# The last part of each query tile's difference goes to GpSimd

## The chip, the cores and the metric

The kernel runs on one core of a Trainium2 chip. The metric is the device time of one execution in microseconds (us). The page and the trace come from one profiled execution. TensorE multiplies and transposes (it writes PSUM alone), VectorE and ScalarE compute element by element in SBUF and PSUM, GpSimd computes in SBUF, and SyncE issues most of the DMAs.

## The reference, cut to what matters

A trunk of two layers over 2048 tokens of width 1024, all in float32: layer 0 runs differential attention (4 heads) and a sliding-window attention side by side, layer 1 a chunked attention. The change lies in the differential attention:

```python
def block(args):                       # one query tile of 128 tokens
    ...
    s = jnp.einsum('bhmqd,bhmkd->bhmqk', qi, k,
                   preferred_element_type=jnp.float32) * ATTN_SCALE + bias
    p = jax.nn.softmax(jnp.where(allowed, s, -jnp.inf), axis=-1)
    attn = p[:, :, 0] - lam * p[:, :, 1]
    return jnp.einsum('bhqk,bhkd->bhqd', attn.astype(v.dtype), v)
```

Each head has two maps m = 0 and 1 of 64 channels each. Their softmaxes are subtracted with the weight lam, and the difference is multiplied with v (128 channels). A query tile i sees the key tiles 0 to i.

## The kernel before, in words

`trunk` runs the stages one after the other: `prepare`, `project`, `diff_attn`, `band_attn` and `output` for layer 0, then `project`, `band_attn` and `output` for layer 1. Each engine has its own instruction list in a stage, and the lists meet at semaphores alone. The change touches `diff_attn`, which lies at 649 to 1090 us of the trace.

`steps` counts the pairs (head h, query tile i) as g = 0 to 63, 16 for each of 4 heads. The row of i + 1 key tiles is cut in two ways. `parts[g, m]` cuts it from the end for the logits, so that the last part holds up to 4 tiles (512 columns) that end on the diagonal. `turns[g]` cuts it from the start in groups of 4 tiles for the difference, the transposes and the product with v, so that the last group holds 1 to 4 tiles. Both have 1 part for i = 0 to 3, 2 for 4 to 7, 3 for 8 to 11 and 4 for 12 to 15.

Round g does the following on each engine, in the order written here.
- TensorE: logits of map 0 (`qk`, L632, two matmuls a part; a part waits until the exponential five parts back has left its PSUM buffer, L629), the product with v of tile g - 2 (`pv`, L658), logits of map 1, then the transposes of tile g - 1 (L645). The transposes of a group wait for its difference (L641) and for one of two PSUM buffers to be emptied (L643).
- VectorE: the minima of map 0 (the logits are negated; L700 for all parts but the last, L707 over these, and L711, which adds the bias to the last part and ends the minimum), the difference of tile g - 1, the minima of map 1, and the output of tile g - 2 (L730).
- ScalarE: the exponentials of map 0 with their sums (L764), the copies of the transposed groups of tile g - 1 to SBUF (L772), the exponentials of map 1, and the squares of tile g - 3 (L778).
- GpSimd: two memsets at the start of the stage (L612, L616), then nothing.

The difference (`difference`, L714 to L726) forms the row sums (L719), their reciprocals (L720) and `ratio`, the number by which map 1 is scaled against map 0 (L721). Then one scalar_tensor_tensor for each group reads both maps from SBUF and writes prob0 + ratio x prob1 over prob0 (L725). The buffers `prob` exist twice, for even and odd g.

Outside this stage GpSimd splits weights into a high and a low part: a cast (L332, L936) and a subtraction (L334, L938). VectorE's L447 is a scalar_tensor_tensor from two SBUF tensors, and L79 and L80 are tensor_tensor operations on one column.

Of the kernel before, what the change touches and what calls it, by code (L numbers as in the profile page):

```python
# [22 lines left out]
ALU = mybir.AluOpType  # L23
# [3 lines left out]
P = 128  # L27
# [496 lines left out]
def diff_attn(nc, before, keep, scr):  # L524

    with ExitStack() as ctx:
# [14 lines left out]
        part_sum = st.sb("part_sum", [P, 2, 2, 4])  # L542
        row_sum = st.sb("row_sum", [P, 2])
        inv_sum = st.sb("inv_sum", [P, 4, 2])
        ratio = st.sb("ratio", [P, 1])
        RING = 5
        logits = [st.ps(f"logits{i}", [P, BLK]) for i in range(RING)]
        turned = [st.ps(f"turned{i}", [P, BLK]) for i in range(2)]
        o_ps = st.ps("o", [P, P])
        head_loaded = [st.sems(f"head_loaded{b}_", NBLK) for b in range(2)]  # L550
        bias_loaded, flipped, bias_made, mask_set, chain = (st.sem(x) for x in ("bias_loaded", "flipped", "bias_made", "mask_set", "chain"))
        qk_done, max_done, exp_done, diff_done, turned_done, prob_t_done, pv_done, out_done, sq_done = (
            st.sem(x) for x in ("qk_done", "max_done", "exp_done", "diff_done", "turned_done", "prob_t_done", "pv_done", "out_done", "sq_done"))
        mean_done, root_done, norm_done, norm_turned, norm_out, stored = (
            st.sem(x) for x in ("mean_done", "root_done", "norm_done", "norm_turned", "norm_out", "stored"))
        LOADS = 13
# [17 lines left out]
        for g, (h, i) in enumerate(steps):  # L574
            turns[g] = []
            for at in range(0, i + 1, TPB):
                turns[g].append((group, at, min(TPB, i + 1 - at)))
                group += 1
        G = len(steps)

        block = ctx.enter_context(nc.Block())

# [26 lines left out]
        @block.gpsimd  # L609
        def _(pool):  # L610
            st.clear_before(pool)
            nc.gpsimd.memset(bias[:, :, 0:BLK - NEAR], 0.0).then_inc(mask_set, 1)  # L612
            pool.wait_ge(mask_set, 1)

            pool.wait_ge(bias_made, A_HEADS // 2)
            nc.gpsimd.memset(bias[0:HD, :, BLK - HD:BLK], MASKED).then_inc(mask_set, 1)  # L616

        @block.tensor
        def _(pe):
            def qk(g, m, k):  # L620

                h, i = steps[g]
                if k >= len(parts[g, m]):
                    return
                if m == 0 and k == 0 and i % TPB == 0:
                    pe.wait_ge(head_loaded[h % 2][i // TPB], 16 * LOADS * (h // 2 + 1))
                n, at, tiles = parts[g, m][k]
                if n >= RING:
                    pe.wait_ge(exp_done, n - RING + 1)  # L629
                for s in range(2):  # L630
                    q = q_sb[h % 2][m][s][:, i * P:(i + 1) * P]
                    last = nc.tensor.matmul(logits[n % RING][:, 0:tiles * P], q, k_sb[h % 2][m][:, at * P:(at + tiles) * P],  # L632
                                            start=s == 0, stop=s == 1)
                last.then_inc(qk_done, 1)

            def transposes(g, k):

                if k >= len(turns[g]):
                    return
                n, at, tiles = turns[g][k]  # L640
                pe.wait_ge(diff_done, n + 1)  # L641
                if n >= 2:
                    pe.wait_ge(prob_t_done, n - 1)  # L643
                for t in range(tiles):
                    last = nc.tensor.transpose(turned[n % 2][:, t * P:(t + 1) * P], prob[g % 2][0][:, (at + t) * P:(at + t + 1) * P], keep["ident"][:, :])  # L645
                last.then_inc(turned_done, 1)

            def pv(g, k):

                h, i = steps[g]  # L650
                if k >= len(turns[g]):
                    return
                n, at, tiles = turns[g][k]
                pe.wait_ge(prob_t_done, n + 1)
                if k == 0 and g >= 1:
                    pe.wait_ge(out_done, g)
                for t in range(at, at + tiles):
                    last = nc.tensor.matmul(o_ps[:, :], prob_t[:, g % 2, t * P:(t + 1) * P], v_sb[:, h % 2, t, :], start=t == 0, stop=t == i)  # L658
                if k == len(turns[g]) - 1:
                    last.then_inc(pv_done, 1)  # L660

            pe.wait_ge(bias_loaded, 16)
            for n in range(A_HEADS // 2):
                nc.tensor.matmul(turned[n % 2][:, :], keep["flip"][:, :], bias_raw[:, 2 * n:2 * n + 2, :], start=True, stop=True).then_inc(flipped, 1)
            pe.wait_ge(bias_made, A_HEADS // 2)
            for g in range(G + 2):
                for k in range(NBLK if g < G else 0):
                    qk(g, 0, k)
                for k in range(NBLK if g >= 2 else 0):
                    pv(g - 2, k)  # L670
                for k in range(NBLK if g < G else 0):
                    qk(g, 1, k)
                for k in range(NBLK if 1 <= g <= G else 0):
                    transposes(g - 1, k)
            for n in range(A_HEADS * NBLK):
                pe.wait_ge(norm_done, TPB * (n + 1))
                if n >= 2:
                    pe.wait_ge(norm_out, n - 1)
                for t in range(TPB):
                    last = nc.tensor.transpose(turned[n % 2][:, t * P:(t + 1) * P], out[:, n * TPB + t, :], keep["ident"][:, :])  # L680
                last.then_inc(norm_turned, 1)

        @block.vector
        def _(dve):
# [29 lines left out]
            def difference(g):  # L714

                h, i = steps[g]
                k = len(parts[g, 0])
                dve.wait_ge(exp_done, parts[g, 1][-1][0] + 1)
                link(nc.vector.reduce_sum(row_sum[:, :], part_sum[:, g % 2, :, 0:k], AX.X))  # L719
                link(nc.vector.reciprocal(inv_sum[:, g % 4, :], row_sum[:, :]))  # L720
                link(nc.vector.scalar_tensor_tensor(out=ratio[:, :], in0=row_sum[:, 0:1], scalar=keep["nlam"][:, 0:1],  # L721
                                                    in1=inv_sum[:, g % 4, 1:2], op0=ALU.mult, op1=ALU.mult))
                for n, at, tiles in turns[g]:
                    cols = slice(at * P, (at + tiles) * P)
                    nc.vector.scalar_tensor_tensor(out=prob[g % 2][0][:, cols], in0=prob[g % 2][1][:, cols], scalar=ratio[:, 0:1],  # L725
                                                   in1=prob[g % 2][0][:, cols], op0=ALU.mult, op1=ALU.add).then_inc(diff_done, 1)  # L726

            def output(g):
# [24 lines left out]
        @block.scalar  # L753
        def _(act):
            def exponentials(g, m):
                j = (2 * g + m) % 4
                act.wait_ge(max_done, 2 * g + m + 1)
                if g >= 2:
                    if m == 0:
                        act.wait_ge(turned_done, turns[g - 2][-1][0] + 1)  # L760
                    else:
                        act.wait_ge(diff_done, turns[g - 2][-1][0] + 1)
                for k, (n, at, tiles) in enumerate(parts[g, m]):
                    nc.scalar.activation(prob[g % 2][m][:, at * P:(at + tiles) * P], logits[n % RING][:, 0:tiles * P], ACT.Exp,  # L764
                                         bias=neg_max[:, j:j + 1], scale=-1.0, accum_out=part_sum[:, g % 2, m, k:k + 1]).then_inc(exp_done, 1)

            def leave(g):
                if g >= 2:
                    act.wait_ge(pv_done, g - 1)
                for n, at, tiles in turns[g]:  # L770
                    act.wait_ge(turned_done, n + 1)
                    nc.scalar.activation(prob_t[:, g % 2, at * P:(at + tiles) * P], turned[n % 2][:, 0:tiles * P], ACT.Copy).then_inc(prob_t_done, 1)  # L772

            def squares(g):
                act.wait_ge(out_done, g + 1)
                if g >= 1:
                    act.wait_ge(sq_done, g)
                nc.scalar.activation(square[:, :], out[:, g, :], ACT.Square, accum_out=ssq[:, g:g + 1]).then_inc(sq_done, 1)  # L778

            for g in range(G + 3):  # L780
                if g < G:
                    exponentials(g, 0)
                if 1 <= g <= G:
                    leave(g - 1)
                if g < G:
                    exponentials(g, 1)
                if g >= 3:
                    squares(g - 3)
            act.wait_ge(mean_done, 1)
            nc.scalar.activation(root[:, :], mean[:, :], ACT.Sqrt).then_inc(root_done, 1)  # L790
            for n in range(A_HEADS * NBLK):
                h, b = divmod(n, NBLK)
                act.wait_ge(norm_turned, n + 1)
                nc.scalar.activation(prob[h // 2][h % 2][:, b * BLK:(b + 1) * BLK], turned[n % 2][:, :], ACT.Copy,
                                     scale=keep["sub_g"][:, 0:1]).then_inc(norm_out, 1)
# [541 lines left out]
```

## Time and profile before

| what | value |
| --- | --- |
| median of 3 runs | 2934.63 us (2934.42 to 2936.46) |
| the profiled execution's own time | 2935.31 us |
| its span in the trace | 2933.6 us |
| mean granted TensorE clock | 0.969 of full speed |
| busy: TensorE matmuls | 2656.7 us (91%) |
| busy: VectorE | 1154.5 us (39%) |
| busy: ScalarE | 1019.0 us (35%) |
| busy: GpSimd | 307.9 us (10%) |

The span runs from the first to the last instruction of the program; the profiled execution's own time is 1.7 us longer. The busy shares are means over stages with different limits: in the first attention VectorE is busy for some 86 us of each 100, in the projections it is nearly idle. Matmuls are pipelined and the ends of their rows are modelled, so a busy TensorE need not be one at its peak. Busy spans of GpSimd are rough.

### The profile page before, as it was taken

Reading aid. Unit: us, or ns where it says so; the run is one execution under the profiler, and the core shown is the slowest. Engines: PE = TensorE matmul, PEld = TensorE weight load, DVE = VectorE, ACT = ScalarE, POOL = GpSimd, SP = SyncE. Lnnn points to the kernel's source line nnn. Section 1 sums busy time; section 2 is a strip of 40 time slices with the busy share of each in tenths; the row PEclk is TensorE's granted clock in tenths of the full one; section 3 lists DMA queues with packets and bytes.
Section 4 is the critical chain, followed back from the end, with each engine's and each line's share of the span. In section 5 each row is a group of like instructions: output and inputs, shape, how many; then the busy total and the mean of one; then the engine's idle time right before and its main releaser. Section 6 shows DMA issues by size and latency. Waiting matters only on the chain. (4 is left out here: it accounts for less than half of the span.)

```text
span 2933.6 us, 44852 instructions
## 1 busy us (share of the span) xinstructions
PE 2656.7 (91%) x16292; PEld 2252.2 (77%) x16292; DVE 1154.5 (39%) x2983; ACT 1019.0 (35%) x2516; POOL 307.9 (10%) x193
## 2 busy tenths in 40 slices
PE   3999999988888876679969999999996999999898
PEld 2788888986677655558858888888995888888687
DVE  5411111108889865445531111111101555555465
ACT  3211111006777754432221111111001777777221
POOL 1121212100000002110011122122100000100100
PEclk9999999999999998889979999999997999999899
DMA  4433322129414028866563433322216677875552
GB/s 140 128 123 107 122 79 82 50 68 182 101 29 74 1 89 188 184 184 225 190 204 108 129 123 114 101 79 70 68 47 154 127 155 156 165 145 123 183 202 85
DMA packets 235396, 358.27 MB, mean 122 GB/s; under 512 B 63464, under 2 KB 132756, under 8 KB 234692
## 3 DMA queue, kind: packets, MB, share of 16 engines
q1 hardware_dynamic: 225140, 316.95, 41.0%
q0 software_dynamic: 10064, 38.80, 4.5%
q8 instruction: 116, 1.90, 0.3%
q14 instruction: 76, 0.62, 0.1%
HBM read 222.45 MB, written 133.21 MB: 121 GB/s over the span
## 5 line engine op out<-in xcount | busy, mean ns | idle before, releaser
L509 PE MATMUL p_acc<-p_h_hi,p_w_hi 128*128 128x512 f32 x1440 | 566.5, 393 | 16.1 <-DVE p_h_lo L457 16.1
L509 PE MATMUL p_acc<-p_h_lo,p_w_hi 128*128 128x512 f32 x1440 | 563.2, 391 | 0.0
L509 PE MATMUL p_acc<-p_h_hi,p_w_lo 128*128 128x512 f32 x1440 | 563.0, 391 | 0.0
L509 PEld LDWEIGHTS p_acc<-p_h_hi,p_w_hi 128*128 128x128 f32 x1440 | 272.0, 189 | 74.6 <-DVE p_h_lo L457 19.4
L509 PEld LDWEIGHTS p_acc<-p_h_hi,p_w_lo 128*128 128x128 f32 x1440 | 271.7, 189 | 56.8
L509 PEld LDWEIGHTS p_acc<-p_h_lo,p_w_hi 128*128 128x128 f32 x1440 | 272.0, 189 | 55.3
L1034 DVE CUSTOM_DVE_ANT_0 c_logits<-c_logits,c_bias 128x640 f32<-128x640 f32 (+4 forms) x256 | 191.5, 748 | 228.7 <-PE c_logits L961 220.7
L305 DVE SCALAR_TENSOR_TENSOR p_lo_out<-p_acc,p_hi_out 128x512 fp32r<-128x512 f32 x116 | 80.2, 691 | 498.3 <-ACT p_hi_out L289 498.3
L289 ACT ACTIVATE p_hi_out<-p_acc 128x512 fp32r<-128x512 f32 x116 | 69.4, 598 | 513.6 <-PE p_acc L509 513.5
L506 PE MATMUL p_acc<-p_w_hi,p_h_lo 128*128 128x256 f32 (+1 forms) x768 | 224.3, 292 | 0.0
L506 PE MATMUL p_acc<-p_w_lo,p_h_hi 128*128 128x256 f32 (+1 forms) x768 | 224.3, 292 | 0.0
L506 PE MATMUL p_acc<-p_w_hi,p_h_hi 128*128 128x256 f32 (+1 forms) x768 | 224.3, 292 | 0.0
L1262 PE MATMUL o_acc<-w_out_hi,o_m_hi 128*128 128x512 f32 x512 | 204.4, 399 | 6.7 <-DVE o_m_lo L1213 6.7
L764 ACT ACTIVATE a_prob<-a_logits,a_neg_max 128x512 f32<-128x512 f32 (+3 forms) x320 | 195.8, 624 | 41.7 <-DVE a_neg_max L711 40.3
L961 PE MATMUL c_logits<-c_k,c_q 128*128 128x384 f32 (+2 forms) x960 | 202.0, 330 | 8.8 <-DMA c_v<-scr_v 6.8
L1262 PE MATMUL o_acc<-w_out_lo,o_m_hi 128*128 128x512 f32 x512 | 201.5, 394 | 0.0
L1262 PE MATMUL o_acc<-w_out_hi,o_m_lo 128*128 128x512 f32 x512 | 201.3, 393 | 0.0
L632 PE MATMUL a_logits<-a_k,a_q 128*128 128x512 f32 (+3 forms) x640 | 175.3, 395 | 27.1 <-ACT a_prob L764 18.4
L1074 ACT ACTIVATE c_prob<-c_logits,c_neg_max 128x640 f32<-128x640 f32 (+4 forms) x256 | 186.2, 727 | 30.8 <-DVE c_neg_max L1034 30.6
L1063 ACT ACTIVATE c_prob_t<-c_turned 128x512 f32<-128x512 f32 (+3 forms) x256 | 141.5, 553 | 115.3 <-PE c_turned L970 115.2
L961 PEld LDWEIGHTS c_logits<-c_k,c_q 128*128 128x128 f32 x960 | 152.9, 191 | 31.7 <-issue 19.0
L988 PE MATMUL c_o<-c_prob_t,c_v 128*64 128x128 f32 x2240 | 168.4, 278 | 8.0 <-DVE c_prob_t L1048 6.5
(161 smaller groups left out, 4036.3 us busy)
## 6 DMA issues: line engine op xcount, KB each, us to landing
scr_qh<-p_hi_out SPq DMA_DIRECT2D x116, 256.0 KB, 2.5
scr_ql<-p_lo_out SPq DMA_DIRECT2D x116, 256.0 KB, 2.9
scr_gt<-p_f_out SPq DMA_DIRECT2D x128, 128.0 KB, 1.9
p_w_raw<-in_w_in_odd POOLq DMA_DIRECT2D x16, 1024.0 KB, 6.7
c_q<-scr_qh SPq DMA_DIRECT2D x64, 256.0 KB, 8.0
c_q<-scr_ql SPq DMA_DIRECT2D x64, 256.0 KB, 9.8
o_o<-scr_ot SPq DMA_DIRECT2D x6, 2048.0 KB, 9.2
o_g<-scr_gt SPq DMA_DIRECT2D x6, 2048.0 KB, 15.0
```

Of the source, the lines that this page charges most:

```text
L289: nc.scalar.activation(hi_out[:, buf, :], ps[:, :], ACT.Copy, scale=kind[1]).then_inc(act_done, 1)
L305: nc.vector.scalar_tensor_tensor(out=lo_out[:, buf, :], in0=ps[:, :], scalar=kind[1], in1=hi_out[:, buf, :].bitcast(F32), op0=ALU.mult, op ...
L506: last = nc.tensor.matmul(acc[v % 4][:, 0:n], ht[:, c, k * P:(k + 1) * P], wt[:, half, c * n:(c + 1) * n], **flags)
L509: last = nc.tensor.matmul(acc[v % 4][:, :], wt[:, half, c * n + cc * P:c * n + (cc + 1) * P], ht[:, c, b * BLK:(b + 1) * BLK], **flags)
L632: last = nc.tensor.matmul(logits[n % RING][:, 0:tiles * P], q, k_sb[h % 2][m][:, at * P:(at + tiles) * P], start=s == 0, stop=s == 1)
L764: nc.scalar.activation(prob[g % 2][m][:, at * P:(at + tiles) * P], logits[n % RING][:, 0:tiles * P], ACT.Exp, bias=neg_max[:, j:j + 1], sc ...
L961: last = nc.tensor.matmul(s_ps[:, lo:hi], q_sb[b][s][:, i * P:(i + 1) * P], k_sb[b][:, tile * P:tile * P + hi - lo], start=s == 0, stop=s ...
L988: last = nc.tensor.matmul(o_ps[half * HD:(half + 1) * HD, at:at + P], v_sb[:, j // TILES % 2, tile_of(j + half) - w + 1 + t, :], prob_t[:, ...
L1034: nc.vector.tensor_tensor_reduce(out=to, in0=s, in1=bias[:, b, WIDE - w * P:WIDE + SPARE], scale=1.0, scalar=HIGHEST, op0=ALU.add, op1=ALU ...
L1063: nc.scalar.activation(prob_t[:, j % 4, 0:n], turned[j % 2][:, 0:n], ACT.Copy).then_inc(main_copied, 1)
L1074: nc.scalar.activation(prob[:, j, 0:n], source, ACT.Exp, bias=neg_max[:, j:j + 1], scale=-1.0, accum_out=sums[:, h, tile_of(k):tile_of(k) ...
L1262: last = nc.tensor.matmul(acc[u % 4][:, :], mt[:, t % 2, c, :], wt[:, c, half * BLK:(half + 1) * BLK], start=step == 0, stop=step == 3 * K ...
```

## The change

For every query tile with more than one group (i = 4 to 15, 48 of 64 tiles), the last group of the difference is no longer formed by VectorE. GpSimd waits for the ratio and the last exponential, scales its columns of map 1 in place by the ratio, waits for its own result, and adds them to map 0. `ratio` gets two columns, one for even and one for odd g, and its writing signals `ratio_set`, on which VectorE waits as well in place of `chain`. The last group's transposes wait for `pool_diff_done`, the others for `diff_done`, whose count is taken over VectorE's groups alone (`owned`). VectorE waits before it writes the ratio, and ScalarE before it writes map 1, for GpSimd's difference of two tiles ago.

```diff
-        ratio = st.sb("ratio", [P, 1])
+        ratio = st.sb("ratio", [P, 2])
...
+        shared = [g for g in range(G) if len(turns[g]) > 1]
+
+        def alone(g):
+            return turns[g][:-1] if g in shared else turns[g]
+
+        owned = {g: sum(len(alone(e)) for e in range(g + 1)) for g in range(G)}
+        lent = {g: sum(e <= g for e in shared) for g in range(G)}
...
             nc.gpsimd.memset(bias[0:HD, :, BLK - HD:BLK], MASKED).then_inc(mask_set, 1)
+            for g in shared:
+                n, at, tiles = turns[g][-1]
+                cols = slice(at * P, (at + tiles) * P)
+                pool.wait_ge(exp_done, parts[g, 1][-1][0] + 1)
+                pool.wait_ge(ratio_set, g + 1)
+                nc.gpsimd.tensor_scalar(prob[g % 2][1][:, cols], prob[g % 2][1][:, cols], ratio[:, g % 2:g % 2 + 1], None, ALU.mult).then_inc(pool_scaled, 1)
+                pool.wait_ge(pool_scaled, lent[g])
+                nc.gpsimd.tensor_tensor(prob[g % 2][0][:, cols], prob[g % 2][0][:, cols], prob[g % 2][1][:, cols], ALU.add).then_inc(pool_diff_done, 1)
...
-                pe.wait_ge(diff_done, n + 1)
+                if g in shared and k == len(turns[g]) - 1:
+                    pe.wait_ge(pool_diff_done, lent[g])
+                else:
+                    pe.wait_ge(diff_done, owned[g] - len(alone(g)) + k + 1)
...
-                link(nc.vector.scalar_tensor_tensor(out=ratio[:, :], in0=row_sum[:, 0:1], scalar=keep["nlam"][:, 0:1],
-                                                    in1=inv_sum[:, g % 4, 1:2], op0=ALU.mult, op1=ALU.mult))
-                for n, at, tiles in turns[g]:
+                if g >= 2 and lent[g - 2] > 0:
+                    dve.wait_ge(pool_diff_done, lent[g - 2])
+                scaled_by = ratio[:, g % 2:g % 2 + 1]
+                nc.vector.scalar_tensor_tensor(out=scaled_by, in0=row_sum[:, 0:1], scalar=keep["nlam"][:, 0:1],
+                                                    in1=inv_sum[:, g % 4, 1:2], op0=ALU.mult, op1=ALU.mult).then_inc(ratio_set, 1)
+                dve.wait_ge(ratio_set, g + 1)
+                for n, at, tiles in alone(g):
...
-                        act.wait_ge(diff_done, turns[g - 2][-1][0] + 1)
+                        act.wait_ge(diff_done, owned[g - 2])
+                        if lent[g - 2] > 0:
+                            act.wait_ge(pool_diff_done, lent[g - 2])
```

## Rows read from the trace of the kernel before

**Rows 1.** Busy time by engine (x instructions) in stretches: tiles 5 and 13.

```profile
core 0: us, PE busy (x) PEld busy (x) DVE busy (x) ACT busy (x) POOL busy (x), PEclk, DMA share, GB/s
784.40:789.00 4.60, 4.08 (x27) 3.15 (x26) 4.41 (x15) 3.83 (x14) 0.00 (x0) 1.00 0.82 219
840.60:851.00 10.40, 8.94 (x59) 7.08 (x58) 8.72 (x23) 7.49 (x22) 0.00 (x0) 1.00 0.00 1
```

**Rows 2.** Timeline, tile 13: start, length, engine, line, operation, [idle before <- releaser].

```profile
845.80 0.90 PE L645 MATMUL a_turned<-keep_ident,a_prob 128*128 128x128 f32 x6 [0.68 <-ACT a_prob_t L772]
...
847.95 0.30 PEld L632 LDWEIGHTS a_logits<-a_k,a_q 128*128 128x128 f32 x2 [1.22 <-ACT a_prob L764]
```

**Rows 3.** Timeline, difference of tile 6 of the second head and what follows.

```profile
789.40 0.22 DVE L721 SCALAR_TENSOR_TENSOR a_ratio<-a_row_sum,keep_nlam,a_inv_sum 128x1 f32<-128x1 f32 x1
789.65 1.28 DVE L725 SCALAR_TENSOR_TENSOR a_prob<-a_prob,a_ratio 128x512 f32<-128x512 f32 x2
...
790.46 0.84 PEld L645 LDWEIGHTS a_turned<-keep_ident,a_prob 128*128 128x128 f32 x7 [0.55 <-DVE a_prob L725]
...
791.29 1.40 PE L632 MATMUL a_logits<-a_k,a_q 128*128 128x128 f32 x6
...
792.42 0.69 ACT L764 ACTIVATE a_prob<-a_logits,a_neg_max 128x512 f32<-128x512 f32 x1 [0.23 <-DVE a_neg_max L711]
...
792.51 0.88 DVE L700 TENSOR_REDUCE a_part_max<-a_logits 128x1 f32<-128x128 f32 x2
...
793.61 0.76 DVE L711 CUSTOM_DVE_ANT_0 a_logits<-a_logits,a_bias,a_part_max 128x512 f32<-128x512 f32 x1
```

**Rows 4.** Timeline, difference of tile 7 of the second head and what follows.

```profile
794.94 1.42 DVE L725 SCALAR_TENSOR_TENSOR a_prob<-a_prob,a_ratio 128x512 f32<-128x512 f32 x2
...
796.41 0.42 PEld L645 LDWEIGHTS a_turned<-keep_ident,a_prob 128*128 128x128 f32 x4 [0.24 <-DVE a_prob L725]
...
798.23 0.37 ACT L764 ACTIVATE a_prob<-a_logits,a_neg_max 128x128 f32<-128x128 f32 x1 [0.53 <-DVE a_neg_max L711]
...
798.74 0.74 PE L632 MATMUL a_logits<-a_k,a_q 128*128 128x512 f32 x2 [0.96 <-ACT a_prob L764]
...
799.63 0.76 DVE L711 CUSTOM_DVE_ANT_0 a_logits<-a_logits,a_bias,a_part_max 128x512 f32<-128x512 f32 x1
```

**Rows 5.** Timeline, difference of tile 15 of the second head, third head's start.

```profile
861.25 2.74 DVE L725 SCALAR_TENSOR_TENSOR a_prob<-a_prob,a_ratio 128x512 f32<-128x512 f32 x4
...
863.55 1.23 PE L645 MATMUL a_turned<-keep_ident,a_prob 128*128 128x128 f32 x8 [0.18 <-ACT a_prob_t L772]
...
864.21 1.20 ACT L772 ACTIVATE a_prob_t<-a_turned 128x512 f32<-128x512 f32 x2 [0.21 <-PE a_turned L645]
...
865.31 0.36 ACT L764 ACTIVATE a_prob<-a_logits,a_neg_max 128x128 f32<-128x128 f32 x1
```

**Rows 6.** Timeline in the first projection, where GpSimd and VectorE meet.

```profile
42.33 1.28 DVE L447 SCALAR_TENSOR_TENSOR p_x<-p_x,p_inv,p_g 128x1024 f32<-128x1024 f32 x1
43.36 2.01 POOL L332 CAST p_w_hi<-p_w_raw 128x2048 fp32r<-128x2048 f32 x1 [7.66 <-DMA p_w_raw<-in_w_in_even]
...
45.45 4.50 POOL L334 TENSOR_TENSOR p_w_lo<-p_w_raw,p_w_hi 128x2048 fp32r<-128x2048 f32 x1
...
47.89 2.08 DVE L79 TENSOR_TENSOR p_root<-p_inv 128x1 f32<-128x1 f32 x1
50.01 0.16 DVE L80 TENSOR_TENSOR p_root<-p_root,p_mean 128x1 f32<-128x1 f32 x1
```

**Rows 7.** Groups of GpSimd by shape: busy, mean ns of one, idle before.

```profile
L334 POOL TENSOR_TENSOR p_w_lo<-p_w_raw,p_w_hi 128x2048 fp32r<-128x2048 f32 x24 | 110.3, 4594 | 2.1
L332 POOL CAST p_w_hi<-p_w_raw 128x2048 fp32r<-128x2048 f32 x24 | 45.5, 1895 | 828.1 <-PE p_acc L509 739.8 <-PE p_acc L506 75.4 <-DMA p_w_raw<-in_w_in_even 7.7
L938 POOL TENSOR_TENSOR w_out_lo<-c_w_raw,w_out_hi 128x1024 fp32r<-128x1024 f32 x8 | 18.9, 2357 | 0.7
...
L1132 POOL COPY o_wide<-o_inv_sums 128x512 f32<-128x512 f32 x16 | 9.8, 614 | 169.3 <-PE o_spread L1247 140.5 <-remote 28.8
```

More of the change, by code:

```diff
@@ L551, in diff_attn @@
         bias_loaded, flipped, bias_made, mask_set, chain = (st.sem(x) for x in ("bias_loaded", "flipped", "bias_made", "mask_set", "chain"))
-        qk_done, max_done, exp_done, diff_done, turned_done, prob_t_done, pv_done, out_done, sq_done = (
-            st.sem(x) for x in ("qk_done", "max_done", "exp_done", "diff_done", "turned_done", "prob_t_done", "pv_done", "out_done", "sq_done"))
+        qk_done, max_done, exp_done, ratio_set, pool_scaled, pool_diff_done, diff_done, turned_done, prob_t_done, pv_done, out_done, sq_done = (
+            st.sem(x) for x in ("qk_done", "max_done", "exp_done", "ratio_set", "pool_scaled", "pool_diff_done", "diff_done", "turned_done", "prob_t_done", "pv_done", "out_done", "sq_done"))
         mean_done, root_done, norm_done, norm_turned, norm_out, stored = (
@@ L720, in difference @@
                 link(nc.vector.reciprocal(inv_sum[:, g % 4, :], row_sum[:, :]))
-                link(nc.vector.scalar_tensor_tensor(out=ratio[:, :], in0=row_sum[:, 0:1], scalar=keep["nlam"][:, 0:1],
-                                                    in1=inv_sum[:, g % 4, 1:2], op0=ALU.mult, op1=ALU.mult))
-                for n, at, tiles in turns[g]:
+                if g >= 2 and lent[g - 2] > 0:
[5 more added lines that the diff above has]
+                for n, at, tiles in alone(g):
                     cols = slice(at * P, (at + tiles) * P)
-                    nc.vector.scalar_tensor_tensor(out=prob[g % 2][0][:, cols], in0=prob[g % 2][1][:, cols], scalar=ratio[:, 0:1],
+                    nc.vector.scalar_tensor_tensor(out=prob[g % 2][0][:, cols], in0=prob[g % 2][1][:, cols], scalar=scaled_by,
                                                    in1=prob[g % 2][0][:, cols], op0=ALU.mult, op1=ALU.add).then_inc(diff_done, 1)
```

## The prediction

> **What bounds the kernel now.** I read the page first: the chain that ended last lies in the last output stage and says nothing of the first attention. So I took the busy time of each engine in stretches as long as one query tile of that attention, then the timeline of single tiles, always asking which engine starts the next piece without having waited. A "step" i below is the stretch after the difference of query tile i; it has ceil((i+1)/4) parts, and its last part has 1 to 4 tiles.
>
> The stage has two regimes. In the two-part steps VectorE is nearly full: 4.41 of 4.60 us [rows 1]. In the four-part steps it is not: 8.72 of 10.40 us [rows 1]. There TensorE waits for ScalarE, which has to empty the two transpose buffers and then free a logits buffer [rows 2]; the last part's difference is ready long before its turn. So a difference that VectorE finishes earlier can be worth something in short steps only, and one that comes ready later hurts where TensorE is already waiting for it: in the two-part steps (0.55 and 0.24 us [rows 3, 4]) and behind tile 15 of a head, where the next head's tile is small and nothing else is left to do.
>
> **What VectorE gets rid of.** 12 tiles of a head (i = 4 to 15) lose their last part. Two parts in a row, the last of 384 columns, take 1.28 us, and with 512 columns 1.42 [rows 3, 4]; four of 512 take 2.74 [rows 5]. So one of 512 costs (2.74 - 1.42)/2 = 0.66 us of slot, one of 384 0.52, and by the same slope 256 and 128 cost 0.39 and 0.26. That is 3 x (0.66 + 0.52 + 0.39 + 0.26) = 5.5 us a head, 22 us in all.
>
> **What GpSimd takes for it.** No row shows its tensor_scalar. From below it costs what the one-input copies cost: 0.614 us at 512 columns and 1.895 at 2048 [rows 7], so 0.83 ns a column over 0.19: 0.61, 0.51, 0.40, 0.29 us for 4 to 1 tiles. From above it costs a tensor_tensor. That has two inputs: 2.357 us at 1024 and 4.594 at 2048 [rows 7], so 2.18 ns a column over 0.12: 1.24, 0.96, 0.68, 0.40 us. I take the copy's price, since the operation has one input tensor as well. Between the two instructions lie 0.08 us (43.36 + 2.01 to 45.45 [rows 6]). The sum is 1.93, 1.55, 1.16, 0.77 us for 4 to 1 tiles. 
>
> **When GpSimd can start.** Both engines wait for the same ratio. VectorE's own next operation starts 0.25 us after the ratio's start [rows 3]; GpSimd cannot be earlier by more than a few hundredths. The rows then show that the two don't run side by side. VectorE's tensor_tensor of one column took 2.08 us instead of the 0.16 of its neighbour, and ended at 49.97, with GpSimd's tensor_tensor that had begun before it and ended at 49.95 [rows 6]. The other way, GpSimd's cast took 2.01 us instead of 1.895 when it began under a scalar_tensor_tensor that reads two SBUF tensors [rows 6, 7], the very form of the difference. In both cases the second one ran as if it had started 0.14 us before the first one's end. So I take it that of a difference on VectorE and an operation on GpSimd the later waits for the earlier. The Trainium skill says so too (SBUF — State Buffer, "Who interferes with whom"): a VectorE instruction with two SBUF inputs and a GpSimd instruction that reads SBUF exclude each other for the whole instruction. It adds that issue order decides who blocks; what happens when a third instruction queues up is shown by no row here.
>
> One part of 512 lasts 0.75 us (1.42 - 0.66 [rows 4]). VectorE's first part begins at 0; GpSimd's scaling then runs from 0.61 on.
>
> **Two-part steps (i = 4 to 7).** VectorE has only that one part, so GpSimd goes on undisturbed and is ready at 0.61 + 0.77, 1.16, 1.55, 1.93 = 1.38, 1.77, 2.16, 2.54 us. VectorE was ready at 1.02, 1.15, 1.28, 1.42, the first two by the slope of the slots and the others from [rows 3, 4]. The last transposes come 0.36, 0.62, 0.88 and 1.12 us later, while VectorE itself arrives earlier at its next maxima and waits there.
> - i = 6 [rows 3]: ready at 789.65 + 2.16 = 791.81. Three weight loads of 0.12 (0.84/7) bring TensorE to the next logits at 792.2 instead of 791.29; its second pair ends about 793.15; a maximum over 512 columns and the small one behind it bring VectorE to its last maximum at 794.1 instead of 793.61: +0.48. So 0.40 of the 0.88 us is covered.
> - i = 5 and 4 have the same order of work; with the same cover 0.62 gives +0.22 and 0.36 gives nothing.
> - i = 7 [rows 4]: ready at 794.94 + 2.54 = 797.48; transposes, copy and with it the exponentials start 0.55 later (798.78 instead of 798.23, since four transposes and a copy need 1.3 us). The logits that wait for the first of them move from 798.74 to 799.29 and end at 800.03 instead of 799.48. VectorE's last maximum, which stood 0.15 behind them at 799.63, can begin at 800.06: +0.43.
>
> Sum of a head +1.13, four heads +4.5 us.
>
> **Steps of three and four parts.** GpSimd finishes before the transposes want it: those of the last part wait for the buffer [rows 2]. The one gain is in step 8, the last one in which VectorE still leads: its slot of 0.26 less a wait of some 0.1 for GpSimd's scaling. I take -0.2 a head, -0.8 us in all. In steps 12 to 14 GpSimd gets between VectorE's parts and costs VectorE 0, 0.3 and 0.54 us net, worked out as for tile 15 below, which its 1.7 idle us of such a step [rows 1] hide; without that cover it would be +0.8 a head.
>
> **Behind tile 15.** Four parts become three on VectorE. If the one that waits first goes first, the order is part, scaling, part, addition, part: scaling ready at 0.61 + 0.61 = 1.22, second part from 1.08 to 1.83, addition from 1.69 to 2.93, third part from 2.79 to 3.54. Before, the third part was ready at 0.75 + 2 x 0.65 = 2.05. Its transposes began at 863.55 and its copy at 864.21 [rows 5], 0.66 apart; now they begin at 861.25 + 3.54 + 0.04 = 864.83, the copy at 865.49: +1.28 us. The fourth follows at once. The next head's exponentials (865.31 [rows 5]) stand behind these copies on ScalarE, and the product with v behind them on TensorE: +1.28 for all that follows, four times +5.1 us.
>
> **The added waits.** VectorE's for the GpSimd difference of two tiles ago, with its own parts and maxima queued behind it, and ScalarE's likewise, fall a whole step (4 us or more) after that difference is done: nothing. GpSimd has nothing else queued in this stage.
>
> **Sum.** 4.5 - 0.8 + 5.1 = +8.8 us. The profiled execution's 2935.3 would become 2944.1; against the median of 2934.6 that is 2943.4 us.
>
> **Rivals.**
> - VectorE keeps the lock between its parts, as its next part is issued before the last has drained. Then GpSimd starts after all of VectorE's parts. The two-part steps are the same (+4.5), step 8 gives its whole 0.26 (-1.0); behind tile 15 the last part is ready at 2.05 - 0.14 + 1.93 = 3.84 instead of 2.74, of which the wait for a transpose buffer hides some 0.1: +1.0 a head, +4.0. Sum +7.5: 2942 us.
> - GpSimd's scaling costs as much as its addition. All of GpSimd's work is longer by 0.63, 0.45, 0.28, 0.11 us, nearly all of it in the open: about 0.1 + 0.3 + 0.45 + 0.6 + 0.65 and 0.3 in step 14, 2.4 a head, +9.5 us more: 2953 us.
> - Not slower: the two engines don't exclude each other for this pair of forms. GpSimd is then ready at 0.03 + 1.93 and so on, behind VectorE's old time by only 0.5 us or less, inside the cover of 0.40 or near it. Steps 4 to 7 then give only about 0.1 each, because the exponentials that the next ratio waits for follow ScalarE's copies and these start no earlier; step 8 gives 0.3 and the head's end 0.4: -1.1 a head, 2930.2 us, within 0.2%. It decides as soon as VectorE's parts keep their 0.66 us spacing with GpSimd busy. The lengthened rows speak against it.
> - Faster: VectorE bounds all steps and the whole 22 us come back: 2912 us. Its idle time in long steps and the waits of TensorE for it in short ones speak against it.
>
> **Chances.** Taking turns as summed 0.50, VectorE's parts first 0.20, dear scaling 0.15, no exclusion 0.10, whole gain 0.05. A measurement of this kernel tells from no change what is over about 0.2% (5.9 us). My terms are 1 us in 4, so the first two cases fall within 5.9 us three times in ten: same 0.21 + 0.09 = 0.30, faster 0.05, slower 0.65. The range leaves out the whole gain and most of no exclusion and reaches up to the dear scaling: 2936 to 2953.
>
> **What would show it.** In the changed profile: GpSimd's scaling of 512 columns ends 1.2 us after VectorE's first part began, not 0.65; in four-part steps VectorE's parts stand over 1 us apart; TensorE's wait before the transposes names GpSimd in steps 5 to 7 of each head and from tile 15's first part to the next head's exponentials it takes 5.3 us instead of 4.1 [rows 5]; the steps with three and four parts keep their length. It is wrong if those long steps get shorter, if the two engines' operations overlap at their usual lengths, or if GpSimd's two instructions at 512 columns last well over 2 us.

## The result and the profile after

The changed kernel takes 2955.61 us (median of 4 runs, 2952.96 to 2958.84) where the kernel before takes 2935.55 (2934.42 to 2936.89): ratio 1.007, 95% interval 1.0057 to 1.0083, so 20 us or 0.7% slower. The forecast was slower, 2943.4 us, range 2936 to 2953. The time lies outside the range, and the loss is more than twice the 8.8 us of the sum. The profiled execution took 2956.68 us, with a span of 2954.9.

In the two traces the first copy of the first attention on VectorE starts 1.6 us earlier than before, and the first matrix multiplication of the next stage 19.3 us later (1114.77, before 1095.52). No other stage changed its length by more than 1.6 us. To see where the loss arose, I took the starts of the row sum (L719 before, L737 after) as marks and compared the length of each step (mark of tile i to mark of tile i + 1) with the same step in the kernel before. The first row gives the length before in us, the others the difference:

| head, step i | 4 | 5 | 6 | 7 | 8 | 9 | 10 | 11 | 12 to 14 | 15 |
| --- | --- | --- | --- | --- | --- | --- | --- | --- | --- | --- |
| second head before | 4.23 | 4.64 | 5.30 | 6.02 | 6.51 | 6.88 | 8.19 | 9.09 | 29.6 | 5.20 |
| first | +0.23 | +0.77 | +1.37 | +1.49 | -0.17 | -0.05 | -0.11 | +0.02 | +0.05 | +0.82 |
| second | +0.22 | +0.76 | +1.22 | +1.46 | -0.13 | -0.05 | -0.09 | -0.02 | +0.03 | +0.82 |
| third | +0.23 | +0.76 | +1.22 | +1.98 | +0.36 | +0.07 | 0.00 | +0.01 | +0.06 | +0.81 |
| fourth | +0.23 | +0.77 | +1.23 | +1.97 | +0.72 | -0.10 | -0.07 | -0.03 | +0.03 | |

Steps 0 to 3 are unchanged to 0.01 us. The two-part steps bear 16 of the 18.9 us between the first mark and the last; of the rest of the stage's loss, 0.6 us lie before the first mark and 1.3 behind the last.

The groups of GpSimd in this stage, by shape (busy, mean ns of one, idle before):

```profile
L629 POOL TENSOR_SCALAR a_prob<-a_prob,a_ratio 128x512 f32<-128x512 f32 x12 | 24.3, 2022 | 62.5 <-ACT a_prob L788 36.6 <-DVE a_ratio L742 25.9
...
L631 POOL TENSOR_TENSOR a_prob<-a_prob 128x512 f32<-128x512 f32 x12 | 15.6, 1301 | 1.0
...
L629 POOL TENSOR_SCALAR a_prob<-a_prob,a_ratio 128x128 f32<-128x128 f32 x12 | 13.0, 1087 | 114.5 <-ACT a_prob L788 114.5
```

The scaling, forecast at 0.61 us for 512 columns, takes longer than the addition. The timeline of tile 7 of the second head, where [rows 4] stood:

```profile
800.59 0.75 DVE L747 SCALAR_TENSOR_TENSOR a_prob<-a_prob,a_ratio 128x512 f32<-128x512 f32 x1
800.73 2.05 POOL L629 TENSOR_SCALAR a_prob<-a_prob,a_ratio 128x512 f32<-128x512 f32 x1 [3.72 <-ACT a_prob L788]
...
802.86 1.26 POOL L631 TENSOR_TENSOR a_prob<-a_prob 128x512 f32<-128x512 f32 x1
...
804.17 0.42 PEld L663 LDWEIGHTS a_turned<-keep_ident,a_prob 128*128 128x128 f32 x4 [2.35 <-POOL a_prob L631]
...
805.11 1.16 DVE L718 TENSOR_REDUCE a_part_max<-a_logits 128x1 f32<-128x256 f32 x2 [1.72 <-PE a_logits L647]
805.36 0.36 ACT L788 ACTIVATE a_prob<-a_logits,a_neg_max 128x128 f32<-128x128 f32 x1
```

The last part is ready 3.53 us after VectorE's first part began (1.42 in [rows 4]); TensorE's weight loads stand idle for 2.35 us (0.24 before), and VectorE, freed 0.66 us earlier, waits 1.72 us for the logits behind those transposes. Tile 15 of the same head, against [rows 5]:

```profile
868.11 2.51 DVE L747 SCALAR_TENSOR_TENSOR a_prob<-a_prob,a_ratio 128x512 f32<-128x512 f32 x3
868.25 2.05 POOL L629 TENSOR_SCALAR a_prob<-a_prob,a_ratio 128x512 f32<-128x512 f32 x1 [6.48 <-DVE a_ratio L742]
868.92 0.42 PEld L663 LDWEIGHTS a_turned<-keep_ident,a_prob 128*128 128x128 f32 x4 [1.20 <-DVE a_prob L747]
...
870.01 0.42 PEld L663 LDWEIGHTS a_turned<-keep_ident,a_prob 128*128 128x128 f32 x4 [0.68 <-DVE a_prob L747]
...
870.38 1.37 POOL L631 TENSOR_TENSOR a_prob<-a_prob 128x512 f32<-128x512 f32 x1
...
871.80 0.42 PEld L663 LDWEIGHTS a_turned<-keep_ident,a_prob 128*128 128x128 f32 x4 [0.71 <-POOL a_prob L631]
...
872.99 0.36 ACT L788 ACTIVATE a_prob<-a_logits,a_neg_max 128x128 f32<-128x128 f32 x1
```

The first and second group of transposes are 1.09 us apart (868.92 and 870.01), not 0.66: VectorE's second part was held, which here means that it ended later than in the kernel before, by 0.43 us, and only by that, though the scaling went on until 870.30.

### The profile page after: what moved, and what is told of

The parts are those of the page before. It is cut to its first block and busy times, and to the rows that moved or that the text cites. A ratio compares the mean times of both kernels' runs of the same rounds, so it can differ in the third digit from the quotient of the medians.

```text
span 2954.9 us, 45009 instructions
## 1 busy us (share of the span) xinstructions
PE 2661.7 (90%) x16292; PEld 2256.1 (76%) x16292; DVE 1148.8 (39%) x2935; ACT 1020.3 (35%) x2516; POOL 428.8 (15%) x289
## 5 line engine op out<-in xcount | busy, mean ns | idle before, releaser
L332 POOL CAST p_w_hi<-p_w_raw 128x2048 fp32r<-128x2048 f32 (+2 forms) x27 | 51.0, 1887 | 931.4 <-PE p_acc L509 844.6
```

Of the source, the lines that this page charges most:

```text
L332: nc.gpsimd.tensor_copy(w_hi[:, s % 2, 0:KC * n], w_raw[:, 0:KC * n]).then_inc(w_hi_done, 1)
```

## The experiments

The first theory after the result: the loss is the late last part in two-part steps and at tile 15, late because the scaling is far dearer than a copy. The rival: VectorE and GpSimd exclude each other, and that is what costs, wherever both work. Kernels are compared with the kernel before in the same runs; its median there was 2937.5 us for the first four, 2934.4 for the next three and 2938.4 for the last.

**What the operations cost alone (e_bench).** `go` issues an operation and waits for its end.

```diff
+                for n in (1, 2, 3, 4):
+                    to, one, two = (trial[:, j, 0:n * P] for j in range(3))
+                    go(nc.gpsimd.tensor_scalar(one, one, scale[:, 0:1], None, ALU.mult))
+                    go(nc.gpsimd.tensor_tensor(to, one, two, ALU.add))
+                    go(nc.gpsimd.tensor_scalar(two, two, 1.0, None, ALU.mult))
+                    go(nc.gpsimd.tensor_copy(to, two))
+                    go(nc.gpsimd.tensor_tensor(one, one, scale[:, 0:1].to_broadcast([P, n * P]), ALU.mult))
```

> The kernel before, with 60 operations of GpSimd on scratch tiles added one after the other in the first stage, where VectorE does nothing that matters: its time as a whole is of no interest, only the length of each operation alone. Theory (the scaling itself is dear): in the changed kernel GpSimd's tensor_scalar by a column of factors ended 1.23, 1.54, 1.87, 2.19 us after VectorE's part began, and could start at 0.61; alone it should take about 0.61, 0.93, 1.25, 1.57 us for 1 to 4 tiles. Rival (the long rows are waits for VectorE, the operation costs as a copy does): 0.29, 0.40, 0.51, 0.61 us. Second rival (no wait is in them at all): 1.09, 1.41, 1.73, 2.05 us. tensor_tensor 0.40, 0.68, 0.96, 1.24 by all of them. Whether a factor that is a constant, or a multiplication by the factor column read as a tensor, is cheaper is open; the column read as a tensor should cost as a tensor_tensor, 1.24 us at 4 tiles.

Groups of GpSimd by shape in this run:

```profile
L172 POOL TENSOR_SCALAR prep_trial<-prep_trial,prep_scale 128x512 f32<-128x512 f32 x3 | 4.7, 1565 | 0.3
L174 POOL TENSOR_SCALAR prep_trial<-prep_trial 128x512 f32<-128x512 f32 x3 | 4.5, 1490 | 0.3
L173 POOL TENSOR_TENSOR prep_trial<-prep_trial 128x512 f32<-128x512 f32 x3 | 3.8, 1262 | 0.2
L172 POOL TENSOR_SCALAR prep_trial<-prep_trial,prep_scale 128x384 f32<-128x384 f32 x3 | 3.7, 1247 | 0.3
...
L176 POOL TENSOR_TENSOR prep_trial<-prep_trial,prep_scale 128x512 f32<-128x512 f32 x3 | 3.1, 1041 | 0.3
...
L172 POOL TENSOR_SCALAR prep_trial<-prep_trial,prep_scale 128x256 f32<-128x256 f32 x3 | 2.8, 924 | 0.3
...
L175 POOL COPY prep_trial<-prep_trial 128x512 f32<-128x512 f32 x3 | 1.8, 611 | 0.2
L172 POOL TENSOR_SCALAR prep_trial<-prep_trial,prep_scale 128x128 f32<-128x128 f32 x3 | 1.8, 605 | 0.3
```

The scaling alone takes 0.605, 0.924, 1.247 and 1.565 us, the theory's four numbers to 0.01. So 2.05 us in the changed kernel are 1.57 of work and 0.48 of waiting, from 0.14 after the start of VectorE's first part to 0.62: the wait behind that part was forecast right, the price was not. A constant factor is hardly cheaper (1.490). Multiplying two tensors is much cheaper (1.041), and cheaper than the 1.24 expected of it. The time of this kernel, 2980.11 us in one run, says nothing: the trial operations are in it.

**Which steps pay (e_two, e_long, e_edge).** Each hands over the last parts of some tiles only:

```diff
-        shared = [g for g in range(G) if len(turns[g]) > 1]
+        shared = [g for g in range(G) if 4 <= steps[g][1] < 8]    (e_two; e_long: 8 <= ... < 15; e_edge: ... == 15)
```

> GpSimd takes the last part of tiles 4 to 7 of each head alone, VectorE does tiles 8 to 15 whole. Theory (the loss is the late last part in the two-part steps): these steps grew by 0.23, 0.77, 1.3 and 1.5 us (2.0 where the TensorE clock fell), 16 to 17 us in four heads: 2951 to 2953 us. Rival (the loss is spread over all shared tiles, as VectorE is slowed by GpSimd wherever both work): 16 of 48 tiles, a third of the 20 us, 2942 us.

> GpSimd takes the last part of tiles 8 to 14 of each head alone. Theory: step 8 gains 0.15 us a head and the rest nothing, though VectorE's parts stand up to 0.43 us apart more: 2935 us, within 1.5 us of the kernel before. Rival (spread loss): 28 of 48 tiles, 2947 us. Rival of another kind (taking work off VectorE is a gain where nothing waits for GpSimd): its 28 parts of 0.26 to 0.66 us, 12 us, 2924 us.

> GpSimd takes the last part of tile 15 of each head alone. Theory: each head's end grows by 0.82 us, the last one perhaps by more: +3.3 to +4 us, 2939 us. Rival (spread loss): 4 of 48 tiles, 2937.5 us. By the sum of the prediction it would be +5.1 us.

| run | median us | ratio to before | 95% interval | marks, first to last |
| --- | --- | --- | --- | --- |
| e_two | 2952.01 | 1.0054 | 1.0036 to 1.0073 | +18.0 us |
| e_long | 2934.70 | 0.9994 | 0.9984 to 1.0003 | -0.8 us |
| e_edge | 2938.56 | 1.0009 | 0.9999 to 1.002 | +2.9 us |

Tiles 4 to 7 alone bring 0.54% of the 0.70%: 16 tiles, a third of those shared, most of the loss. In e_two their steps grow by 0.22, 0.77, 1.23 and 1.5 to 2.0 us as in the changed kernel, 15.8 of its 18.0 us; 1.6 of the rest lie in step 8, where GpSimd does nothing in this run, and 0.6 in one early step. Tiles 8 to 14 cost nothing and gain nothing that their time can tell; the marks of e_long show step 8 shorter by 0.15 us in three heads (longer by 0.09 in the fourth), steps 9 and 10 by 0.05 and 0.1 us. In e_edge tile 15 adds 0.82, 1.04 and 0.81 us in the three heads that have a mark behind it; the time of that run alone couldn't tell 2937.5 us from 2939. So "spread over all shared tiles" falls, and so does "work taken off VectorE is a gain where nothing waits for GpSimd".

**A cheaper scaling (e_add).**

```diff
-                nc.gpsimd.tensor_scalar(prob[g % 2][1][:, cols], prob[g % 2][1][:, cols], ratio[:, g % 2:g % 2 + 1], None, ALU.mult)...
+                nc.gpsimd.tensor_tensor(prob[g % 2][1][:, cols], prob[g % 2][1][:, cols], ratio[:, g % 2:g % 2 + 1].to_broadcast([P, tiles * P]), ALU.mult)...
```

> The changed kernel, with GpSimd's scaling written as a multiplication of two tensors, the second one the factor column repeated over the width. Theory (the length of GpSimd's two operations after VectorE's part is what the two-part steps pay): if this form costs 0.40, 0.68, 0.96, 1.24 us instead of 0.61, 0.93, 1.25, 1.57, the last part comes earlier by 0.21, 0.25, 0.29, 0.33 us, nearly all of it in steps 5 to 7 and at tile 15: about 1.1 to 1.4 us a head, 5 us in all, so 2950 to 2951 us where the changed kernel takes 2955.6. Rival (the lock on VectorE's second part is what counts): two inputs hold it longer, so this is no faster, 2955 us or more.

Measured: 2954.75 us, ratio 1.0067 (1.004 to 1.0094), which can't be told from the changed kernel; by the marks +16.7 us instead of +18.9. The two-part steps of the second head grow by 0.01, 0.45, 0.79 and 0.93 us (0.22, 0.76, 1.22, 1.46 in the changed kernel): each pays less by what the last part is earlier. But step 15 of the first head grows by 1.54 us instead of 0.82. An operation of GpSimd that reads two inputs holds VectorE's parts longer (second head):

```profile
864.16 3.87 DVE L747 SCALAR_TENSOR_TENSOR a_prob<-a_prob,a_ratio 128x512 f32<-128x512 f32 x3
864.27 1.54 POOL L629 TENSOR_TENSOR a_prob<-a_prob,a_ratio 128x512 f32<-128x512 f32 x1 [7.01 <-DVE a_ratio L742]
...
865.89 1.59 POOL L631 TENSOR_TENSOR a_prob<-a_prob 128x512 f32<-128x512 f32 x1
```

VectorE's three parts take 3.87 us here, 2.51 in the changed kernel. In the second and third heads step 15 grows by more, 2.37 and 1.69 us, and the step behind it by 0.73 and 1.40. There the granted clock fell to 1.2 GHz for 3.4 us (from 868.1 and 973.9), behind waits of TensorE of 1.0 us for VectorE's parts (columns as in [rows 1]):

```profile
864.00:868.00 4.00, 2.08 (x16) 1.47 (x14) 3.96 (x5) 1.31 (x4) 3.14 (x2) 1.00 0.00 2
868.00:872.00 4.00, 3.91 (x21) 3.91 (x22) 1.82 (x10) 2.29 (x8) 0.00 (x0) 0.57 0.00 0
```

Against the first head, where the clock stayed up, that is about 3.1 us of the 16.7. The two-part steps save 7.2 us in all, and tile 15 gives 3.2 of them back, part of it by the clock. So theory and rival are both right in kind, each in its steps, and the theory's 2950 to 2951 us missed what happens at tile 15.

**The exclusion by itself (e_shadow, e_fill).** VectorE forms all parts as before, and GpSimd works beside it on scratch tiles:

```diff
+        shade = st.sb("shade", [P, 2, BLK])
...
-                nc.gpsimd.tensor_scalar(prob[g % 2][1][:, cols], prob[g % 2][1][:, cols], ratio...
+                nc.gpsimd.tensor_scalar(shade[:, 1, 0:tiles * P], shade[:, 1, 0:tiles * P], ratio...    (e_fill: nc.gpsimd.memset(shade[:, 1, 0:tiles * P], 1.0))
...
-                for n, at, tiles in alone(g):
+                for n, at, tiles in turns[g]:
```

> VectorE forms every part itself, as in the kernel before, and nothing waits for GpSimd but the writing of the ratio two tiles later; GpSimd does its two operations at the same moments on scratch tiles. So this is the price of the contention alone. Theory (small): VectorE's second part is held 0.11, 0.22, 0.32, 0.43 us, as in the changed kernel, and its later ones by the addition; in two-part steps that delay is under the cover of 0.40 us, at tile 15 a few tenths stay open: 0 to +3 us, 2935 to 2938 us. Rival (contention is the loss): most of the 20 us, 2950 us.

> As the run with scratch tiles, but GpSimd writes constants instead: two operations that read nothing. If it is the reading that excludes VectorE's two-input operation, VectorE's parts keep their distance of 0.65 to 0.67 us in every step and the time is that of the kernel before, 2935 to 2936 us. If any operation of GpSimd excludes it, the second part is held here too, by up to 0.5 us.

e_shadow took 2953.05 us, ratio 1.0063 (1.0043 to 1.0083): my 0 to +3 us was far off. e_fill took 2933.18 us, ratio 0.9994 (0.9983 to 1.0004): these operations, which read nothing, cost nothing, and neither do the signals and waits around the ratio, which both runs keep. Tile 6 and tile 15 in e_shadow, then tile 15 in e_fill:

```profile
790.96 1.61 DVE L748 SCALAR_TENSOR_TENSOR a_prob<-a_prob,a_ratio 128x512 f32<-128x512 f32 x2
791.09 1.74 POOL L633 TENSOR_SCALAR a_shade<-a_shade,a_ratio 128x384 f32<-128x384 f32 x1 [2.61 <-DVE a_ratio L743]
...
864.60 4.19 DVE L748 SCALAR_TENSOR_TENSOR a_prob<-a_prob,a_ratio 128x512 f32<-128x512 f32 x4
864.73 2.06 POOL L633 TENSOR_SCALAR a_shade<-a_shade,a_ratio 128x512 f32<-128x512 f32 x1 [6.89 <-DVE a_ratio L743]
```

```profile
860.44 2.74 DVE L748 SCALAR_TENSOR_TENSOR a_prob<-a_prob,a_ratio 128x512 f32<-128x512 f32 x4
860.52 0.53 POOL L633 MEMSET a_shade<- 128x512 f32 x1 [8.73 <-DVE a_ratio L743]
```

The two parts of tile 6 take 1.61 us instead of 1.28 [rows 3], the four of tile 15 4.19 instead of 2.74 [rows 5]; under the memsets they keep 2.74. The memsets are shorter as well (0.53 us), but the first runs beside VectorE's first part and the second one, from 0.66 to 1.18 us, beside its second, and neither part shows it. e_shadow's profiled execution was its fastest, 14.4 us longer than before by the marks: 4.4 in the two-part steps, 5.8 in steps 8 to 14 and 4.1 at tile 15. By the marks the steps of the second head grow by 0.11, 0.23, 0.32, 0.42 (4 to 7), 0.31, 0.23, 0.21, 0.10 (8 to 11), 0.43 (14) and 1.37 us (15). In the two-part steps this is the hold of the second part, to 0.02 us. VectorE leads there, so its own delay is paid in full; the cover (what a step does not pay of a delay) of 0.40 us that I had applied belongs to a last part that comes late while VectorE itself is early. That is why the expectation was wrong, and the run doesn't contradict the others: the changed kernel has no second part on VectorE in those steps that could be held, and in the steps from 8 on the part that VectorE loses is as long as the hold or longer (0.26 to 0.66 against 0.11 to 0.43 us).

**A law for the two-part steps (e_tile).** In each two-part step take how much later the last part is ready than before, and what the step grows:

| step | ready before | changed: ready, growth | e_add: ready, growth | lateness less growth, both |
| --- | --- | --- | --- | --- |
| 4 | 1.02 | 1.77, 0.22 | 1.55, 0.01 | 0.53, 0.52 |
| 5 | 1.15 | 2.35, 0.76 | 2.03, 0.45 | 0.44, 0.43 |
| 6 | 1.28 | 2.94, 1.22 | 2.51, 0.79 | 0.44, 0.44 |
| 7 | 1.42 | 3.53, 1.46 | 2.99, 0.93 | 0.65, 0.64 |

Ready is counted in us from the start of VectorE's first part. With these two prices of GpSimd's work the cover of a step is the same. To test this forward, GpSimd got one key tile only:

```diff
-        shared = [g for g in range(G) if len(turns[g]) > 1]
+        shared = [g for g in range(G) if 4 <= steps[g][1] < 8]
...
-            return turns[g][:-1] if g in shared else turns[g]
+            if g not in shared:
+                return turns[g]
+            n, at, tiles = turns[g][-1]
+            return turns[g][:-1] + ([(n, at, tiles - 1)] if tiles > 1 else [])
...
-                cols = slice(at * P, (at + tiles) * P)
+                cols = slice((at + tiles - 1) * P, (at + tiles) * P)
...
+                    pe.wait_ge(diff_done, owned[g])
                     pe.wait_ge(pool_diff_done, lent[g])
```

> In tiles 4 to 7 of each head GpSimd takes one key tile (128 columns) of the last part and VectorE the 0 to 3 others; all other tiles are VectorE's alone. Theory (a two-part step grows by how much later its last part is ready than in the kernel before, less a fixed cover): GpSimd is ready 1.77 us after VectorE's first part began in all four steps, instead of 1.02, 1.15, 1.28 and 1.42; the changed kernel and the run with two tensors both gave covers of 0.52, 0.43, 0.44 and 0.64. So the steps should grow by 0.23, 0.19, 0.05 and 0 us, 1.9 us in four heads: 2937 us, a few tenths less for what VectorE is rid of. Rival (what GpSimd and VectorE do to each other's reads counts, whatever is late): VectorE's second part is held 0.11 us in three of the four steps, so each grows by about 0.11 more, and by less in step 4 than in step 7. Second rival (any work of GpSimd there costs as in the run with tiles 4 to 7 whole): 2952 us.

The steps grew by 0.24, 0.19, 0.06 and -0.03 us in the second head and by the same within 0.02 in the others: the law's four numbers. GpSimd's rows there (scaling, addition, by group):

```profile
L632 POOL TENSOR_SCALAR a_prob<-a_prob,a_ratio 128x128 f32<-128x128 f32 x16 | 17.4, 1085 | 314.2 <-ACT a_prob L792 289.9 <-DVE a_ratio L746 24.3
L634 POOL TENSOR_TENSOR a_prob<-a_prob 128x128 f32<-128x128 f32 x16 | 7.3, 454 | 1.3
```

The time was 2936.87 us, ratio 1.0003 (0.9991 to 1.0016): an unchanged time and the 1.9 us of the law (1.0006) both lie inside the interval, the rival's 2952 us far outside. The law rests on the marks, not on this ratio. The first rival is not put to the test by this run, because VectorE was not late in it. Its second part was held by 0.11 us, but it was shorter by one tile, and the two parts of tile 7 end no later than in [rows 4] (1.42):

```profile
793.72 1.39 DVE L751 SCALAR_TENSOR_TENSOR a_prob<-a_prob,a_ratio 128x512 f32<-128x512 f32 x2
```

What a delay of VectorE costs is shown by e_shadow.

**What is left.** Step 7 of the third and fourth heads grew by 1.98 instead of 1.46, and step 8 by 0.36 and 0.72 instead of -0.15. Busy time and granted clock around that step of the third head (columns as in [rows 1]):

```profile
905.00:909.00 4.00, 1.88 (x13) 1.30 (x12) 2.42 (x7) 1.64 (x6) 3.00 (x2) 1.00 1.09 201
909.00:913.00 4.00, 3.96 (x18) 3.04 (x17) 2.81 (x9) 3.35 (x12) 0.19 (x1) 0.57 1.08 226
913.00:917.00 4.00, 3.60 (x26) 2.99 (x24) 3.47 (x9) 2.69 (x8) 1.44 (x2) 1.00 0.32 59
```

TensorE was busy for 1.88 of the 4 us before, and from 909.2 the granted clock was at its lower level of 1.2 GHz for 3.4 us. It was so at three places in this stage of the changed kernel (694.1, 909.2 and 1015.0), behind waits for GpSimd of 1.5, 2.1 and 2.1 us, and at none in the kernel before between 674 and 1072. Step 7 of the second head had the same wait of 2.1 us and no fall, so the wait alone doesn't decide it. The extra is 1.0 us in the third head and 1.4 in the fourth, about 2.4 us in all, and 0.2 in the first. e_two repeats it: the clock fell in step 7 of its first and third heads (701.2 and 909.4), and there alone step 7 grew by 1.98 instead of 1.47 to 1.48 us. That the wait has a part in bringing the clock down is argued from its place; no run separated the two. Pauses of 0.3 to 0.6 us in single steps of some runs (step 8 of the second head of e_two, the third step of its first head) have no cause that the trace shows.

No version beat the kernel before by what a measurement can tell; e_long comes nearest, with 0.8 us by its marks.

## Why the prediction was wrong

- **What bounds the steps: right.** Two-part steps and tile 15 pay, the others don't: the growth in steps 8 to 14 lies between -0.17 and +0.07 us, but for step 8 behind the falls of the clock in the third and fourth heads.
- **What GpSimd takes: the step that failed.** The scaling was priced by the nearest one-input row, 0.61 us at 512 columns; it takes 1.565. The addition was right (1.24 forecast, 1.262 measured). The price of an addition, which the prediction set as the most that it could cost, was no bound: the scaling is dearer than that by 0.3 us. With the same number of inputs a copy costs 0.611 us and the multiplication by a column 1.565, and the estimate of 0.44 us of body that stood beside the copy's price is a third of the 1.28 us that the rows show (2.5 ns a column). The prediction's own sign of being wrong came true: GpSimd's two instructions at 512 columns last 3.39 us from start to end (800.73 to 804.12), well over 2. The rival "dear scaling" (0.15) with 2953 us comes within 3 us of the result, in part by luck: it has 10.3 us in the two-part steps, which pay 14.6 before the clock, and 7.7 at tile 15, which pays 0.82 a head.
- **When GpSimd can start: right.** Behind VectorE's first part, 0.62 us after its start (0.61 forecast).
- **Two-part steps: the method held, with the wrong term in it.** Covers of 0.40 and 0.69 us forecast, 0.53, 0.44, 0.44 and 0.65 measured. With the true price the last part is 0.75, 1.20, 1.66 and 2.11 us late and the steps pay 3.7 us a head, 14.6 in all, where I had 4.5. That is 10 of the 11 us missed. The falls of the clock add some 2.5, and tile 15, forecast too high, takes nearly 2 off.
- **Behind tile 15: near by luck.** Forecast +1.28, measured +0.82 us. I let the second part wait until the scaling ends. It is held for 0.107 us per 128 columns only; the third part then runs at once, and the last one, by GpSimd, sets the end (ready at 3.64 instead of 2.74). The two errors work against each other: with the true price of 1.57 us and a wait until its end, the third part would have been ready at 4.50 us and the same working would have given +2.2 us a head.
- **Steps of three and four parts: right.** Forecast -0.8 us, marks of e_long -0.8 us; its time can't tell that from nothing.
- **The order of turns: right for three parts.** First part, scaling, second part; then whichever asked first: at tile 12 the addition came before the third part, at tiles 13 to 15 after it. The rival "VectorE keeps the lock" falls, since its second part was held in every shared step that has one.
- **No exclusion, the rival within 0.2%:** falls by e_shadow against e_fill, and by the held parts in the changed kernel itself.
- **Range and chances.** The dear price stood among the rivals with 0.15, and the range ended at that rival's time, with no room for a price beyond the assumed bound or for a fall of the clock.

How much of the loss the exclusion itself bears can only be argued from the law: had GpSimd not waited its 0.48 us, the two-part steps would pay 0, 0.3, 0.7 and 1.0 instead of 0.22, 0.76, 1.22 and 1.46 us. So its wait would bear a bit less than half of their loss and the price of its operations the rest. This was not run.

## What to carry to other kernels

Before work moves to GpSimd, count what stands behind it: here a part that came late was paid for microsecond by microsecond beyond a cover of 0.4 to 0.65 us, while freeing VectorE of some 12 us of work in the longer steps gave back 0.8 by the marks of e_long, since it already had idle time there. In the two-part steps its next input hangs on that same part. Take an operation's price from a row of the very same operation, not from one with the same number of inputs; without such a row leave the upper end of the range open. And look at whether both engines read SBUF at the same moment: here VectorE's two-input operations and GpSimd's reads held each other up, and with work on scratch tiles alone that cost 0.63%.

## What the runs showed of the hardware

- GpSimd alone, float32: multiplication by a factor column 0.605, 0.924, 1.247, 1.565 us for 128 to 512 columns (2.5 ns a column), by a constant 1.490 at 512; multiplication of two tensors 1.041, addition of two 1.262, copy 0.611.
- The hold on VectorE's next two-input part follows what GpSimd reads, not how long it runs. Beside the scaling (one input) the second part was held by 0.11, 0.22, 0.32 and 0.43 us for 1 to 4 tiles, while the operation itself grows by 0.32 us a tile; beside the multiplication of two tensors by 0.14, 0.35, 0.57 and 0.78 us. This agrees with the Trainium skill, SBUF — State Buffer, "Who interferes with whom", in what excludes what: a read against a two-input operation, and no memset (e_fill: 0.53 us for 512 columns beside VectorE's part, no part of VectorE longer). It differs where that section lets the loser block for the whole instruction: beside the scaling of 512 columns VectorE went on 1.1 us before that operation ended.
- The granted clock fell to 1.2 GHz for 3.4 us at three places of a stage in which it had held 2.4 GHz, each behind a wait of TensorE for GpSimd of 1.5 to 2.1 us, though only behind three of eight such waits. In e_add it fell twice behind a wait of 1.0 us for VectorE. The step in which it fell and the next one together took 1.0 to 1.4 us more in the changed kernel where it fell in step 7.
